# Half of the experts' weight loads moved from SyncE's DMA queue to GpSimd's

## The reference

```
for layer in range(2):
    mix = ab_mixer(h, ...) if layer % 2 == 0 else dsa_mixer(h, positions, ...)
    h = layer_norm(ALPHA * h + mix, ln_mix_g[layer], ln_mix_b[layer])
    ffn = moe_ffn(h, router_w, router_bias, w_gate[layer], w_up[layer], w_down[layer])
    h = layer_norm(ALPHA * h + ffn, ln_ffn_g[layer], ln_ffn_b[layer])

def moe_ffn(x, ...):                       # 16 experts, 2 per token, width 512
    comb = weights of the two chosen experts of each token, 0 for the others
    hg = einsum('btd,edf->btef', x, w_gate)
    hu = einsum('btd,edf->btef', x, w_up)
    h = silu(hg) * hu * comb[..., None]
    return einsum('btef,efd->btd', h, w_down)
```

## Time and profile before

| | |
|---|---|
| time, median of 3 runs | 1818.32 us (1816.82 to 1819.84) |
| the profiled execution's own time | 1820.55 us |
| its span, first to last instruction | 1818.7 us |
| TensorE busy | 1621.8 us (89%) |
| VectorE busy | 712.4 us (39%) |
| ScalarE busy | 461.0 us (25%) |
| GpSimd busy | 20.5 us (1%), 37 instructions |
| mean granted clock of TensorE | 0.963 |
| bytes read from HBM | 534.80 MB, 295 GB/s over the span |

### The profile page before, as it was taken

One profiled execution on the slowest core, in us unless ns is written; L12 is line 12 of the kernel. 1 busy time (PEld: TensorE's weight loads), 2 busy tenths in 40 slices (PEclk: granted clock), 3 DMA queues, 4 the chain that ended last, 5 costly groups with the idle time before them and its releaser, 6 DMA issues.

```text
span 1818.7 us, 18314 instructions
## 1 busy us (share of the span) xinstructions
PE 1621.8 (89%) x7239; PEld 968.0 (53%) x7239; DVE 712.4 (39%) x1183; ACT 461.0 (25%) x679; POOL 20.5 (1%) x37
## 2 busy tenths in 40 slices
PE   8999999997898888998769989789899988989975
PEld 6888887775433244333258877558653322533322
DVE  6675565656111112111175686435631111121115
ACT  4565545432100001000024344533311000100000
POOL 1000000000000000000000000000000000000000
PEclk9999999998999999999969999989899999999997
DMA  8666555775999999999926345337579999999994
GB/s 263 175 184 184 163 149 152 255 291 208 372 422 421 421 422 421 409 421 421 417 91 190 111 140 171 106 105 270 226 277 414 422 421 421 422 415 421 422 421 194
DMA packets 127273, 538.07 MB, mean 296 GB/s; under 512 B 17764, under 2 KB 17864, under 8 KB 76504
## 3 DMA queue, kind: packets, MB, share of 16 engines
q1 hardware_dynamic: 126616, 532.73, 76.9%
q0 software_dynamic: 576, 4.19, 0.6%
HBM read 534.80 MB, written 2.10 MB: 295 GB/s over the span
## 4 chain that ended last, share of the span: by engine, by line
PE 55%; issue 29%; DMA 9%; DVE 5%; ACT 2%; SPq 0%; POOL 0%; POOLq 0%; DVEq 0%; ACTq 0%
PE ps L703 11%; PE ps L705 11%; PE ps L704 11%; PE ps L973 9%; DMA ring<-in_moe_w_down 6%; PE ps L1027 4%; DMA ring<-in_moe_w_up 3%; PE ps L953 1%; PE ps L670 1%; PE ps L954 1%; PE ps L1118 1%; PE ps L1104 1%; PE ps L1083 1%; DVE arena L2110 1%; PE ps L962 1%
## 5 line engine op out<-in xcount | busy, mean ns | idle before, releaser
L703 PE MATMUL ps<-w_lo,x_hi 128*128 128x512 f32 x896 | 354.2, 395 | 7.3 <-DVE attn_lo L2168 3.0
L1528 DVE TENSOR_TENSOR w_lo<-ring,w_hi 128x1024 fp32r<-128x1024 f32 x224 | 269.8, 1222 | 207.8 <-ACT w_hi L1164 206.3
L704 PE MATMUL ps<-w_hi,x_hi 128*128 128x512 f32 x896 | 350.4, 391 | 0.0
L1164 ACT ACTIVATE w_hi<-ring 128x1024 fp32r<-128x1024 f32 x224 | 235.2, 1059 | 312.4 <-PE ps L705 312.4
L1976 DVE TENSOR_TENSOR arena<-ps,arena 128x512 f32<-128x512 f32 x128 | 83.0, 685 | 408.0 <-PE ps L963 407.9
L703 PEld LDWEIGHTS ps<-w_lo,x_hi 128*128 128x128 f32 x896 | 169.2, 189 | 47.8 <-DVE attn_lo L2168 4.6
L704 PEld LDWEIGHTS ps<-w_hi,x_hi 128*128 128x128 f32 x896 | 168.9, 189 | 35.1
L973 PE MATMUL ps<-arena,hT 128*64 128x512 f32 x768 | 177.9, 619 | 7.8 <-issue 5.0
L1027 PE MATMUL ps<-ring,arena 128*64 128x512 f32 x768 | 170.1, 594 | 12.3 <-DMA ring<-in_moe_w_down 12.3
L1370 ACT ACTIVATE y_hi<-ps 128x512 fp32r<-128x512 f32 x64 | 36.5, 596 | 501.8 <-PE ps L963 263.2
L705 PE MATMUL ps<-w_hi,h_lo 128*128 128x512 f32 x384 | 150.0, 391 | 0.0
(11 more groups left out here) (319 smaller groups left out, 1576.8 us busy)
## 6 DMA issues: line engine op xcount, KB each, us to landing
arena<-in_moe_w_gate SPq DMA_DIRECT2D x48, 2048.0 KB, 17.8
ring<-in_moe_w_down SPq DMA_DIRECT2D x48, 2048.0 KB, 20.5
arena<-in_moe_w_up SPq DMA_DIRECT2D x32, 2048.0 KB, 19.7
ring<-in_moe_w_up SPq DMA_DIRECT2D x32, 2048.0 KB, 20.1
ring<-in_ab_w_in SPq DMA_DIRECT2D x96, 512.0 KB, 3.7
ring<-in_moe_w_gate SPq DMA_DIRECT2D x16, 2048.0 KB, 19.3
arena<-in_moe_w_down SPq DMA_DIRECT2D x16, 2048.0 KB, 19.1
ring<-in_c_w_in SPq DMA_DIRECT2D x64, 512.0 KB, 3.7
```

What stands on the lines that cost most here:

```text
L703: nc.tensor.matmul(t, x_h, w_l[:, k, :], start=(opens and k == 0), stop=False)
L704: nc.tensor.matmul(t, x_h, w_h[:, k, :], start=False, stop=False)
L1164: act.activation(high_unit(n), raw_unit(n)[0], ACT.Copy).then_inc(w_hi_ready, 1)
L1528: v.tensor_tensor(lo, raw, high_unit(n).bitcast(FP32), ALU.subtract).then_inc(w_lo_ready, 1)
```

## The change

Steps with an odd number that are not among a layer's first six are issued by GpSimd, in its own queue, and counted in semaphores of their own (`loaded_odd`). SyncE keeps steps 0 to 5 of the first pair and all even steps. The condition for issuing a step is the same as before. TensorE waits for the semaphore that belongs to the step. GpSimd's loads stand in its stream between the powers of the first and the second norm, and it reads the number of rounds as SyncE does.

```diff
+            s["loaded_odd"] = [sem(f"expert_odd_step_loaded_{lay}_{b}") if b % 2 else None for b in range(6)]
...
+        def load_step(eng, lay, e, x, st):
+
+            if not (isinstance(x, int) and x == 0 and st < 6):
+                eng.wait_ge(M[lay]["step_used"], STEPS * x + st - 5)
+            eng.dma_start(step_slot(st).rearrange("p (e f) -> p e f", e=2), step_source(lay, e, st))\
+               .then_inc(M[lay]["loaded" if eng is nc.sync else "loaded_odd"][st % 6], 16)
...
-                for st in range(4, STEPS):
-                    load_step(lay, 0, 0, st)
+                for st in (4, 5, *range(6, STEPS, 2)):
+                    load_step(sp, lay, 0, 0, st)
                 with sp.Fori(1, PAIRS) as x:
-                    for st in range(STEPS):
-                        load_step(lay, 2 * x, x, st)
+                    for st in range(0, STEPS, 2):
+                        load_step(sp, lay, 2 * x, x, st)
...
                 rstd_step(2 * lay)
+                for st in range(7, STEPS, 2):
+                    load_step(pool, lay, 0, 0, st)
+                with pool.Fori(1, PAIRS) as x:
+                    for st in range(1, STEPS, 2):
+                        load_step(pool, lay, 2 * x, x, st)
+                pool.wait_ge(routed, lay + 1)
+                n_r = pool.value_load(rounds_i[0:1, 0:1], min_val=0, max_val=MAX_ROUNDS - 1) + 1
...
                 rstd_step(2 * lay + 1)
...
-                    pe.wait_ge(s["loaded"][st % 6], 16 * (2 * x + st // 6 + 1))
+                    if st % 2 == 0 or (isinstance(x, int) and x == 0 and st < 6):
+                        pe.wait_ge(s["loaded"][st % 6], 16 * (2 * x + st // 6 + 1))
+                    else:
+                        pe.wait_ge(s["loaded_odd"][st % 6], 16 * (2 * x + st // 6))
```

More of the change, by code:

```diff
@@ L484, in scatter_at, with step_source @@
             return (8 if first else 12) + 4 * (i - 1) + c
+        def step_source(lay, e, st):
+            experts = slice(e, e + 2) if isinstance(e, int) else bass.ds(e, 2)
+            if st < 8:
+                return (gate_w, up_w)[st % 2][lay, experts, st // 2].rearrange("e p f -> p e f")
+            return down_w[lay, experts].rearrange("e p f -> p e f")[:, :, (st - 8) * HALF:(st - 7) * HALF]
+        def load_step(eng, lay, e, x, st):
[3 more added lines that the diff above has]
+               .then_inc(M[lay]["loaded" if eng is nc.sync else "loaded_odd"][st % 6], 16)
         @block.sync
@@ L527, in load_late @@
                 sp.dma_start(router_w[:, :, :], a["router_w"].rearrange("(k p) e -> p k e", p=P)).then_inc(late_loaded, 16)
[L529 to L541, removed]
             def wait_last_pair(st):
@@ L567, in _ @@
                         sp.wait_ge(mix_ready if lay == 0 else mixer1_done, 1)
-                        load_step(lay, 0, 0, (n - UNITS[lay] + 12) // 4)
+                        load_step(sp, lay, 0, 0, (n - UNITS[lay] + 12) // 4)
                 wait_unit_used(sp, lay, UNITS[lay] - RAW + 3)
-                load_step(lay, 0, 0, 3)
+                load_step(sp, lay, 0, 0, 3)
                 wait_unit_used(sp, lay, UNITS[lay] - 1)
-                for st in range(4, STEPS):
-                    load_step(lay, 0, 0, st)
+                for st in (4, 5, *range(6, STEPS, 2)):
+                    load_step(sp, lay, 0, 0, st)
                 with sp.Fori(1, PAIRS) as x:
-                    for st in range(STEPS):
-                        load_step(lay, 2 * x, x, st)
+                    for st in range(0, STEPS, 2):
+                        load_step(sp, lay, 2 * x, x, st)
                 sp.wait_ge(routed, lay + 1)
@@ L582, in _ @@
                         with sp.Fori(0, PAIRS) as y:
-                            for st in range(STEPS):
-                                load_step(lay, 2 * y, r * PAIRS + y, st)
+                            for st in range(0, STEPS, 2):
+                                load_step(sp, lay, 2 * y, r * PAIRS + y, st)
                 load_ffn_ln(lay)
@@ L653, in _ @@
                 rstd_step(2 * lay)
+                for st in range(7, STEPS, 2):
[5 more added lines that the diff above has]
+                n_r = pool.value_load(rounds_i[0:1, 0:1], min_val=0, max_val=MAX_ROUNDS - 1) + 1
+                with pool.If(n_r > 1):
+                    with pool.Fori(1, n_r) as r:
+                        with pool.Fori(0, PAIRS) as y:
+                            for st in range(1, STEPS, 2):
+                                load_step(pool, lay, 2 * y, r * PAIRS + y, st)
                 rstd_step(2 * lay + 1)
@@ L1022, in pair @@
                         st = 8 + j
-                        pe.wait_ge(s["loaded"][st % 6], 16 * (2 * x + 2))
+                        if st % 2 == 0:
+                            pe.wait_ge(s["loaded"][st % 6], 16 * (2 * x + 2))
+                        else:
+                            pe.wait_ge(s["loaded_odd"][st % 6], 16 * (2 * x + 1))
                         w = step_slot(st).rearrange("p (e n) -> p e n", e=2)
```

## The result

The changed kernel takes 1829.76 us (median of 4 runs, 1828.66 to 1831.47), the one before 1817.95 us in the same session (4 runs, 1816.82 to 1819.84): ratio 1.006, 95% interval 1.0046 to 1.0074. That is 11.8 us slower; 1828.7 us was forecast. The profiled execution took 1829.53 us, its span is 1827.9 us.

What follows compares the result with a forecast made beforehand. The weight stream at 421 GB/s was taken as the limit, except where the queue runs dry; 2 layers x 2 places x 2.6 = 10.4 us on 1820.55 gave 1831 profiled, median 1828.7, range 1818 to 1840.

Steps and rivals of the forecast that it cites:

- The sharing: Experts' weight stream: both queues get equal records, each half the rate while both have work; 7 to 20 us slower, chance 0.58.
- Rival 1: Experts' stream: engines take whole steps in turn, order kept; 0 to 2 us, 1818 to 1820; chance within a shared 0.21.
- Rival 2: GpSimd's queue is slower, 414 GB/s against 421; 7.6 us on top of 10.4, 1836, up to 1846; chance 0.14.
- rival 3: Experts' stream: mixing queues fills engines better, 433 GB/s against 421; gains 25 us less 10.4, 1804; chance 0.07.
- Rival 4: GpSimd waits for the first norm's variance and issues step 7 late; at most 1 us; chance within a shared 0.21.
- The size at a place: Delay paid at each of two places per layer: 2.6 us, bounds 1.8 to 5.0.
- f: Lead of the even queue in steps; a pair of steps is late by the larger of 3.5 - 4.98f and 4.98f.
- The starved first pair costs nothing new: Pair 0 of the experts: TensorE waits for no data, a never-idle stream moves the same bytes; 0 us.
- Place 1: Entry to pair 4, the second gathering: entered 2.6 us later, dry spell grows as much; 0 if a reserve hides.
- Place 2: End of the experts' stage: last odd step late because the final norm's 2 MB keep its rate at half; 2.6 us.
- So the formula for the odd step holds to the end: Step 11 of pair 7, with the norm's 2 MB in q1: 2.6 us later, 1.8 to 5.0; without them some 0.9.
- The issues: GpSimd's issue of 2 MB takes 0.6 to 1.2 us beside the transfer; taken as 0, 1 us kept.

## Why the prediction was right

**The sharing: right.** Equal records, not whole steps, now shown with rows of unequal size and by the order of the records. Rival 1 falls with it. Rival 2 falls with all steps in q0 at 421 GB/s and a ratio of 1.0008, rival 3 with the plateaus at 419 to 422. Rival 4 has nothing for it: GpSimd issues step 7 of layer 0's pair 0 in its turn, and TensorE's first wait for data is for an odd step in pair 1 or later, as forecast.

**The size at a place: too small.** The forecast took 2.6 us, the middle of 1.8 (f = 0.36) and 3.3 (f = 0.66). The lead can be read from the landings: an odd step lands 9.95f us behind its even one. In pair 3 of layer 0 that is 5.82 us, so f = 0.585 and the delay 2.9 us. In layer 1 the same two steps are only 4.41 us apart, which makes f 0.44 and the delay 2.2 us:
```profile
1528.45 3.65 PE L989 MATMUL ps<-arena 128*64 128x512 f32 x16 [1.88 <-DMA arena<-in_moe_w_gate]
1532.86 3.65 PE L989 MATMUL ps<-arena 128*64 128x512 f32 x16 [0.75 <-DMA arena<-in_moe_w_up]
```
Measured at the entry are 3.4 us in both. So the term that was mis-sized, 2.6 us at a place, misses in two ways. In layer 0 the lead did not shrink to 0.36 (by the landings in the trace it is 0.79 early in pair 5, behind the dry spell, and 0.62 from step 8 of that pair to the end); and the formula itself falls short, by 0.5 and 1.2 us. For that the prediction has a term that it put at nothing: "The starved first pair costs nothing new". At the end of pair 0, in 16 us, the rate is lower than before (first row after, second before):
```profile
484.00:500.00 16.00, 14.10 (x69) 5.21 (x66) 1.46 (x4) 3.94 (x5) 1.43 (x2) 0.98 0.98 395
484.00:500.00 16.00, 14.10 (x69) 4.97 (x65) 1.16 (x4) 4.24 (x5) 0.00 (x0) 0.99 1.00 419
```
In layer 1 it is 399 GB/s (1373 to 1389 us) against 424 (1370 to 1386). That is 0.9 us of the stream in each layer, of the size of what the formula lacks; that it is the same microsecond is argued, not shown. The full 3.3 us at each place would have given 13.2 us.

**Place 1: right.** The entry is late, the dry spell grows by 3.1 and 2.6 us (2 to 3 forecast), and the half with two queues in pairs 0 to 3 alone keeps 3.0 and 2.0 us of it to the end of the stage.

**Place 2: right in size, wrong in its reason.** This is the step that failed: "So the formula for the odd step holds to the end", because of the norm's 2 MB. The delay is there (2.6 and 2.5 us beyond place 1; 3.7 and 3.0 alone), but without those 2 MB it stays. In place of it the trace shows that the stage's end is no longer bound by the last step. Step 7 is late (888.63 against 881.34, 7.3 us). The four steps behind it are there when TensorE comes to them, and its own work takes 912.15 - 888.63 = 23.5 us, where the stream gave them in 902.60 + 3.65 - 881.34 = 24.9. Only 1.4 us is regained by that. More would be if step 7's products took 3.65 us and not 5.25, but only 0.5 us more: then TensorE would wait for step 11, which lands at 908.1, and the norm's rows would decide, as forecast. That case was not run.

The forecast sum was 10.4 us for four places. Measured are 12.0, in four shares of 2.5 to 3.4, within each place's bounds of 1.8 to 5.0. In the medians it is 11.8. The forecast of the time is off by 1.1 us, of which the starting point and the shares each have a part. That it is so close is partly luck: the bounds for place 2 came from a reason that is wrong, and what holds there instead happens to be of the same size.

**The issues.** GpSimd takes 0.71 us for 2 MB (rows above), in the estimate of 0.6 to 1.2, and nothing waits for it. Of the up to 0.7 us a place that the prediction allowed for a load held back by a VectorE copy, nothing is seen: with all 90 loads of a layer on GpSimd beside these copies the ratio is 1.0008 (0.9998 to 1.0018). The copies of the earlier trace rows read from `ps`, and a copy from SBUF to SBUF was not tried.

## What to carry to other kernels

Where few slots are in flight and the reader takes tiles in order, a second queue doesn't add bandwidth; it lets the tile behind take half of the rate from the tile needed next. If two queues are wanted, give both a part of the same tile (here that still cost a ratio of 1.0014), and don't hand a stream over to another queue while the first still holds older loads. And price a later landing only where the reader has no reserve: here at two places in a layer, and there a landing made a little earlier gains as well.

## What the runs showed of the hardware

- Two queues take turns by single records: 1456 of 1469 records were followed by one of the other queue, from 560 to 600 us. With rows of 8 KB and 4 KB it was 67 against 66 records in 2 us, so the rates stood 2 to 1.
- Rows of 4 KB were slower: when q0 alone was busy with them, from 602 to 604 us, its rate was 410 GB/s against 421 to 422 with rows of 8 KB.
```profile
DMA packets 210, 0.82 MB, mean 410 GB/s; under 512 B 10, under 2 KB 10, under 8 KB 210
```
- A step's 16 products sometimes took 5.2 to 5.4 us instead of 3.65, here behind waits of 2.17, 2.37 and 2.56 us. Windows over step 5 and step 7 of pair 3, after:
```profile
635.10:640.40 5.30, 4.84 (x22) 1.50 (x24) 0.00 (x0) 0.00 (x0) 0.71 (x1) 1.00 1.02 424
645.00:650.30 5.30, 5.30 (x17) 1.48 (x17) 0.00 (x0) 0.00 (x0) 0.00 (x0) 0.68 1.02 424
```
  The granted clock is 1.00 behind a wait of 1.57 us and 0.68 behind one of 2.17, a mixture of the levels of 2.4 and 1.2 GHz (3.65 / 0.68 = 5.4 us). It doesn't follow every such wait; step 7 of pair 2 kept 3.65 us:
```profile
585.38 3.65 PE L989 MATMUL ps<-arena 128*64 128x512 f32 x16 [2.19 <-DMA arena<-in_moe_w_up]
```
